# Order of the weight products within half a slot: chunk by chunk, or output bank by output bank

## The reference, cut to what matters

```python
proj = h @ w_in                                  # mla_mixer, rglru_mixer
out @ w_o
g, u = jnp.split(h @ w_gu, 2, axis=-1)           # swiglu, twice
(jax.nn.silu(g) * u) @ w_down
proj = jnp.einsum('bsd,dc->bsc', h, w_in[layer]) # second_block, two layers
x = x + jnp.einsum('bsc,cd->bsd', y, w_out[layer])
```

## Time and profile before

| what | value |
|---|---|
| median of 3 executions | 3152.2 us (3151.22 to 3152.9) |
| the profiled execution's own time | 3153.71 us |
| its span, first to last instruction | 3151.9 us |
| mean granted TensorE clock | 0.999 |
| TensorE matmul busy | 3132.8 us, 25944 instructions |
| TensorE weight load busy | 3105.1 us, 25944 instructions |
| VectorE busy | 1858.2 us |
| ScalarE busy | 1604.6 us |
| DMA, mean busy share of the 16 engines | 55.8% for the hardware queue |

### The profile page before, as it was taken

The page is one execution under the profiler, slowest core; times in us unless marked ns, Lnnn a source line. Parts: engine busy times, 40 slices in busy tenths (PEclk is TensorE's granted clock), DMA queues, the critical chain, the costliest instruction groups (busy, mean ns, idle before and its releaser), DMA issues.

```text
span 3151.9 us, 60408 instructions
## 1 busy us (share of the span) xinstructions
PE 3132.8 (99%) x25944; PEld 3105.1 (99%) x25944; DVE 1858.2 (59%) x2027; ACT 1604.6 (51%) x2083; POOL 0.2 (0%) x4
## 2 busy tenths in 40 slices
PE   8999999999999999999999999999999999999999
PEld 8999999999999999999999999999999999999999
DVE  6655555445554577765554455547667666656664
ACT  6654433333334366754443344447556655656663
POOL 0000000000000000000000000000000000000000
PEclk9999999999999999999999999999999999999999
DMA  7335555645556555555565555656556556655654
GB/s 228 120 125 173 174 175 175 198 158 174 173 173 202 155 178 175 178 188 187 187 207 184 166 187 187 210 168 168 168 163 177 170 162 187 176 171 167 172 158 146
DMA packets 530768, 551.10 MB, mean 175 GB/s; under 512 B 15296, under 2 KB 524352, under 8 KB 529472
## 3 DMA queue, kind: packets, MB, share of 16 engines
q1 hardware_dynamic: 530624, 549.00, 55.8%
HBM read 541.56 MB, written 2.10 MB: 172 GB/s over the span
## 4 chain that ended last, share of the span: by engine, by line
PE 97%; ACT 1%; DVE 1%; issue 0%; DMA 0%; SPq 0%; ACTq 0%; DVEq 0%
PE ps L640 89%; PE ps L707 2%; PE ps L1062 1%; PE ps L976 1%; PE ps L775 1%; PE ps L967 0%; PE ps L984 0%; PE ps L943 0%; PE ps L883 0%; PE ps L780 0%; PE ps L806 0%; PE ps L939 0%; PE ps L816 0%; PE ps L977 0%; ACT w_hi L1090 0%
## 5 line engine op out<-in xcount | busy, mean ns | idle before, releaser
L640 PE MATMUL ps<-x_hi,w_hi 128*128 128x256 f32 (+1 forms) x5840 | 1653.1, 283 | 11.7 <-DVE w_lo L1741 10.5
L640 PE MATMUL ps<-x_lo,w_hi 128*128 128x256 f32 (+1 forms) x5840 | 1651.8, 283 | 0.0
L640 PE MATMUL ps<-x_hi,w_lo 128*128 128x256 f32 (+1 forms) x5840 | 1647.3, 282 | 0.0
L640 PEld LDWEIGHTS ps<-x_hi,w_hi 128*128 128x128 f32 x5840 | 1100.5, 188 | 18.0 <-issue 14.9
L640 PEld LDWEIGHTS ps<-x_lo,w_hi 128*128 128x128 f32 x5840 | 1098.3, 188 | 0.9
L640 PEld LDWEIGHTS ps<-x_hi,w_lo 128*128 128x128 f32 x5840 | 1098.7, 188 | 0.0
L1606 DVE TENSOR_TENSOR w_lo<-raw,w_hi 128x1024 fp32r<-128x1024 f32 (+3 forms) x496 | 651.2, 1314 | 574.5 <-ACT w_hi L1097 574.2
L1097 ACT ACTIVATE w_hi<-raw 128x1024 fp32r<-128x1024 f32 (+3 forms) x496 | 560.3, 1131 | 706.2 <-PE ps L640 686.7
L1600 DVE TENSOR_TENSOR w_lo<-raw,w_hi 128x1024 fp32r<-128x1024 f32 (+2 forms) x496 | 595.5, 1202 | 488.4 <-ACT w_hi L1090 483.9
L1090 ACT ACTIVATE w_hi<-raw 128x1024 fp32r<-128x1024 f32 (+2 forms) x496 | 513.4, 1037 | 384.2 <-PE ps L640 379.9
L640 PE MATMUL ps<-hid_hi,w_lo 128*128 128x272 f32 (+1 forms) x1408 | 401.0, 285 | 0.0
(11 more groups left out here) (291 smaller groups left out, 2276.7 us busy)
## 6 DMA issues: line engine op xcount, KB each, us to landing
raw<-ffn_w_gu_dram SPq DMA_DIRECT2D x176, 1024.0 KB, 5.1
raw<-w_in_dram SPq DMA_DIRECT2D x128, 1024.0 KB, 5.5
raw<-ffn_w_down_dram SPq DMA_DIRECT2D x64, 1408.0 KB, 6.5
raw<-w_out_dram SPq DMA_DIRECT2D x32, 1024.0 KB, 5.4
raw<-lru_w_in_dram SPq DMA_DIRECT2D x24, 1024.0 KB, 5.5
raw<-mla_w_o_dram SPq DMA_DIRECT2D x16, 1024.0 KB, 5.3
raw<-lru_w_o_dram SPq DMA_DIRECT2D x16, 1024.0 KB, 5.4
raw<-lru_y_gates_dram SPq DMA_DIRECT2D x8, 1280.0 KB, 5.6
```

The source lines that it names most:

```text
L640: mm = pe.matmul(out, l, r, start=first and k == 0 and i == 0, stop=last and k == kn - 1 and i == 2)
```

## The change

Within a half of a slot the two loops change places: the loop over the output banks is now outside, the loop over the chunks inside. The first bank gets all chunks of the half (12 matmuls for 4 chunks), then the second bank gets the same chunks. `at_chunk` is called only during the first bank's turn. The waits on `lo_half` and `lo_made` stay at the head of the halves, `slot_half` at the end of the first half, `slot_done` at the end of the slot. The latent projections (line 707), the recurrence's gates (line 883) and the late half of the output projection (line 1062) have their own loops and are not touched.

```diff
                 half = 4 if kn == 11 else kn // 2
-                for k in range(kn):
-                    if k == 0:
-                        pe.wait_ge(lo_half, n + 1 + 4 * rn)
-                    if k == half:
+                for part, ks in enumerate((range(half), range(half, kn))):
+                    pe.wait_ge(lo_made if part else lo_half, n + 1 + 4 * rn)
+                    for out, c in outs:
+                        for k in ks:
+                            if at_chunk is not None and out is outs[0][0]:
+                                at_chunk(k0 + k)
+                            x_of = (a_hi[:, k0 + k, :], a_lo[:, k0 + k, :])
+                            if ahead is not None and k0 + k < 4:
+                                x_of = (ahead[:, 0, k, :], ahead[:, 1, k, :])
+                            for i, (w, x) in enumerate(((hi, x_of[0]), (hi, x_of[1]), (lo, x_of[0]))):
+                                l, r = (x[:, c], w[:, k, :]) if moving_weights else (w[:, k, c], x)
+                                mm = pe.matmul(out, l, r, start=first and k == 0 and i == 0,
+                                               stop=last and k == kn - 1 and i == 2)
+                    if not part:
                         mm.then_inc(slot_half, 1)
-                        pe.wait_ge(lo_made, n + 1 + 4 * rn)
-                    if at_chunk is not None:
-                        at_chunk(k0 + k)
-                    x_of = (a_hi[:, k0 + k, :], a_lo[:, k0 + k, :])
-                    if ahead is not None and k0 + k < 4:
-                        x_of = (ahead[:, 0, k, :], ahead[:, 1, k, :])
-                    for out, c in outs:
-                        for i, (w, x) in enumerate(((hi, x_of[0]), (hi, x_of[1]), (lo, x_of[0]))):
-                            l, r = (x[:, c], w[:, k, :]) if moving_weights else (w[:, k, c], x)
-                            mm = pe.matmul(out, l, r, start=first and k == 0 and i == 0,
-                                           stop=last and k == kn - 1 and i == 2)
                 if more:
                     mm = more()
                 mm.then_inc(slot_done, 1)
```

## The result

The changed kernel takes 3174.34 us (median of 4, 3173.58 to 3175.45) against 3152.55 us (median of 4, 3151.22 to 3153.62): slower by 21.8 us, ratio 1.0069, 95% interval 1.0056 to 1.0082. The profiled execution took 3174.06 us, its span is 3172.3, 20.4 us longer than the span before.

The account below looks back on a forecast made before the run. TensorE was taken as the bound, fed everywhere, time being matmul count times pace. Terms +1 + 0 + 0 + 0.1 = +1.1 us turned the profiled 3153.71 into 3154.8 us, forecast median 3153.3; range 3147 to 3167 us.

Parts of the forecast that it names:

- What bounds the kernel: Whole kernel: TensorE is fed everywhere, busy 99% of the span, so time is the number of matmuls times their pace.
- the very windows that the prediction named as its sign: Line 637: 322 matmuls per 40 us at 400, 344 to 345 at 1420 and 1800; 340 or 341 there shows slower rival.
- Order of banks, 272 columns: 8,304 matmuls of 272 columns: the new order, judged by line 707's pace, costs +1 us, within 2.5 us either way.
- Order of banks, 256 columns: 256-column matmuls, 11,328 with x: the new order costs 0 us, with bounds of +15 and -13 us.
- the fast stretch needs six matmuls on one chunk: Slower rival, 256-column matmuls with x: pace falls to hid's, +11 to +15 us, 3163 to 3167 us; chance 0.17.
- Waits on chunks: TensorE asks for a new activation chunk every 3 matmuls instead of 6, but chunks are ready in time: cost 0.
- Value matmuls: They come nine matmuls earlier, start near 227 us and wait about 0.1 us for ScalarE's last copy: +0.1 us.
- The faster rival: The excess falls, as bank changes may cost something at 256 columns or the fast stretch grows: -13 us, 3139 us; chance 0.09.
- The stretch that might grow: 256-column matmuls with x: the 114 ns pace might hold for 16 of 24 matmuls instead of about 8: -13 us.

Follow-up runs that it names:

- e15: Kernel before the change, with the second and third activation chunk of each half slot exchanged, six matmuls in a row on a chunk as before: 3161.36 us.
- e8: Kernel before the change, with x_hi and x_lo 32 bytes further on in SBUF and everything behind them 256 bytes further on: 3164.94 us.
- e13: e9 with the chunks of the 256-column stages all beginning at remainder 64 modulo 256 bytes: 3130.28 us.
- e10: The changed kernel with the packing of e9, x chunks of the 256-column stages 1024 bytes apart: 3192.81 us.
- e9: Kernel before the change, with x_hi and x_lo chunks of the 256-column stages packed 1024 instead of 1088 bytes apart, remainder 128: 3183.97 us.
- e3: Kernel before the change, with only the PSUM bank following the new sequence; activation chunks and weight tiles keep the old one: 3152.68 us.
- e17: e13 with the second feed-forward network's hidden activations packed 1024 bytes apart too; hid_hi, hid_lo and head_hl begin at remainder 64: 3141.99 us.
- e14: e9 with the chunks of the 256-column stages all beginning at remainder 192 modulo 256 bytes: 3150.21 us.
- e16: The changed kernel with the packing of e13, remainder 64: 3139.16 us.
- e11: e9 with x_hi and x_lo 128 bytes further on, so that every packed chunk begins at a multiple of 256 bytes: 3170.24 us.
- e6: Kernel before the change, with passes and banks exchanged inside a chunk, the passes in their old order: 3153.18 us.
- e5: Kernel before the change, passes and banks exchanged inside a chunk, passes reordered so four of six matmuls repeat the moving operand: 3155.35 us.
- e1: Kernel before the change, with only the activation chunks read in the new sequence; weight tiles and PSUM banks keep the old one: 3173.92 us.
- e12: The changed kernel with the packing and 128-byte shift of e11: 3178.47 us.

## Why the prediction was wrong

**What bounds the kernel: right.** TensorE is fed everywhere, its waits did not grow, and the time is the count times the pace. All of the loss is pace. It shows in the very windows that the prediction named as its sign: 319 for 322 at 400 us, 341 for 345 and 344 at 1420 and 1800.

**Order of banks, 272 columns: the step that failed first.** I took the pace of line 707 for that of line 637 in the new order, 125.4 ns, and let it cost 1 us. Line 637 now has 126.1 to 126.3, +1.1 to +1.2 ns, some 7 us on 6,192 matmuls of x, where the term allowed 0.3 ns. Line 707 was no control: it differs in order, but its activations are also other tensors at other addresses (`c_hi`, `c_lo`), and the pace depends on that: e15 moves the pace at 272 columns by as much as the new order does (319 a window) through the sequence of the chunks' beginnings alone, and e8 does the same at 256 columns (341) by a shift. Which property of `c_hi` and `c_lo` makes line 707 faster stays open. Line 706 still has its own 125.4 beside it.

**Order of banks, 256 columns: the wrong value was taken within the right bounds.** The bounds stood at +15 and -13 us; I took 0 because the 272-column comparison showed nothing, and that comparison was the first error again. The measured term, 11 to 15 us by the short windows, lies at the upper bound, with +1.4 ns in the feed-forward stage, a little over the 1.3 that the bound was worked out from. The argument beneath it, that a gain which belongs to an address is there in every visit, is refuted by e13: one address has two paces.

**The rival "the fast stretch needs six matmuls on one chunk"** came nearest, with the right direction and the right term at 256 columns, at a chance of 0.17. It had no term for the 272-column stages, so its 3163 to 3167 us and the end of the range, 3167, were 7 to 11 us short of 3174. Its mechanism as I put it, the length of the run, is refuted by e15 and e10, so that its 256-column term came out right is in part luck: hid's pace, which it took for the new one, is one of several that x can have (120.2 ns in e9).

**Waits on chunks: right, 0** (0.6 us in all on `x_lo` at the tight place, 0.7 before). **Value matmuls: right** in that they cost next to nothing: 0.1 us of wait forecast, none seen. They started at 226.10 instead of near 227, since the whole slot came 0.83 us earlier (224.89 for 225.72). **The faster rival** by banks falls with e3. The stretch that might grow is real as a possibility: in e13 it fills whole stages, but the new order does not bring it about.

**The range** left out the case that both the 272-column and the 256-column term go against the forecast. They came from one assumption, that another stage's pace can be carried over, so they had to fail together, and the range should have held their sum: 2.5 + 15 us is 3170, and with the 272-column excess bounded by the largest difference of pace that the earlier trace rows show (1.3 ns, on 8,304 matmuls, 11 us) it would have been 3178.

## What to carry to other kernels

Where TensorE is the bound and never waits, an order of matmuls is not neutral because count, bytes and waits are equal: the distance between starts moved by 1 to 6% with where the moving operands begin and in what sequence they come, here 0.7% of the kernel for an exchange of two loops. A pace read from one stage is weak evidence for another stage whose operand addresses or steps differ, as line 707's was for line 637, and e13 shows two paces even where they are the same. Pads of some tens of columns and packed chunks are a cheap thing to try and to measure, the whole kernel each time, since e17 changed nothing in how the stage at 1780 reads x and its pace changed all the same.

## What the runs showed of the hardware that I had not expected

With 256 moving columns of 4 bytes at the same granted clock, paces of 113.5 and 117.8 ns (both in e13, e14, e16 and e17), 118.8 (e11) and 120.2 (e9), each held through a whole stage. The PSUM bank and the sequence of the weight tiles made no difference to 0.1%, nor did the passes' order on x (e6). In e5 it did on the hidden activations: 338 matmuls in the window at 1650, where the kernel before has 341:

```profile
1650.00:1690.00 40.00, 40.00 (x338) 1.00 0.59 191
```

With chunks 1024 bytes apart, moving the start of x by multiples of 64 bytes gave 3183.97, 3170.24, 3130.28 and 3150.21 us (remainders 128, 0, 64, 192 modulo 256). Whether 256 bytes is the period, whether a state is carried between matmuls, and what picks between the two paces was not tried and stays open; so does the reason why the old sequence of uneven chunks is faster than the new one. What is shown is that the loss comes from the sequence in which the activation's chunks are read (e1), that at 256 columns it vanishes when all chunks begin at one remainder, 128 or 0 (e9 to e12), and that it acts through the pace alone.
